# Stick-breaking attention on Trainium2: a scan over sigmoids with queries in rows, in place of triangle products with keys in rows

## The reference, cut to what matters

```python
def stick_breaking_mixer(x, w_in, w_out):
    q, k, v, g = jnp.split(x @ w_in, 4, axis=-1)          # 16 heads x 64 each
    ...
        z = jnp.einsum('bqhd,bshd->bhqs', qb, k) * HEAD_DIM_2 ** -0.5
        before = pos[None, :] < pb[:, None]
        log_one_minus = jnp.where(before, jax.nn.log_sigmoid(-z), 0.0)
        log_stick = lax.cumsum(log_one_minus, axis=3, reverse=True) - log_one_minus
        a = jnp.where(before, jnp.exp(jax.nn.log_sigmoid(z) + log_stick), 0.0)
        return jnp.einsum('bhqs,bshd->bqhd', a, v)
    ...
    return (o * jax.nn.silu(g)) @ w_out
```

## Time and profile before

| what | value |
|---|---|
| time, median of 3 runs | 1710.23 us (1708.13 to 1712.81) |
| time of the profiled execution | 1712.11 us |
| its span, first to last instruction | 1710.3 us |
| TensorE busy | 1618.1 us, 95% |
| VectorE, ScalarE, GpSimd busy | 873.2, 560.6, 547.1 us |
| TensorE's mean granted clock | 0.978 of full |

### The profile page before, as it was taken

One profiled execution on the slowest core, in us unless ns is written; L12 is line 12 of the kernel. 1 busy time (PEld: TensorE's weight loads), 2 busy tenths in 40 slices (PEclk: granted clock), 3 DMA queues, 4 the chain that ended last, 5 costly groups with the idle time before them and its releaser, 6 DMA issues.

```text
span 1710.3 us, 19912 instructions
## 1 busy us (share of the span) xinstructions
PE 1618.1 (95%) x7794; PEld 1317.4 (77%) x7794; DVE 873.2 (51%) x1604; ACT 560.6 (33%) x1165; POOL 547.1 (32%) x662
## 2 busy tenths in 40 slices
PE   6999999889999899999999998999989898999997
PEld 5888888677777788888788776877777686888885
DVE  2999957356643333333201134984772523655545
ACT  3223341455521222222100013015662205656550
POOL 3222235211124344444444441441102241222221
PEclk9999999899999899999999998999999999999999
DMA  8999988523359688888888884884315584554555
GB/s 232 191 192 190 195 189 192 104 59 75 75 116 225 152 183 190 192 194 193 173 192 177 177 190 85 188 194 86 71 30 135 122 190 95 111 111 99 111 115 131
DMA packets 69277, 253.15 MB, mean 148 GB/s; under 512 B 7616, under 2 KB 7744, under 8 KB 69184
## 3 DMA queue, kind: packets, MB, share of 16 engines
q0 software_dynamic: 66528, 242.25, 66.1%
q1 hardware_dynamic: 2112, 7.53, 1.2%
q10 hardware_dynamic: 544, 2.10, 0.3%
HBM read 249.75 MB, written 2.10 MB: 147 GB/s over the span
## 4 chain that ended last, share of the span: by engine, by line
PE 87%; DVE 5%; ACT 3%; DMA 2%; issue 2%; POOL 0%; SPq 0%; DVEq 0%; ACTq 0%
PE PSUM L426 26%; PE PSUM L428 26%; PE PSUM L427 26%; PE PSUM L707 2%; PE PSUM L586 2%; DMA W_LO<-wstream 2%; PE PSUM L607 2%; PE PSUM L689 1%; PE PSUM L692 1%; DVE MASK L1711 1%; PE PSUM L574 1%; DMA SMALLS<-small 1%; ACT PROBS L927 1%; PE PSUM L617 0%; ACT QKV L904 0%
## 5 line engine op out<-in xcount | busy, mean ns | idle before, releaser
L414 POOL DMA_DIRECT2D W_HI<-wstream x231 | 129.4, 560 | 1008.8 <-PE PSUM L428 1008.3
L426 PE MATMUL PSUM<-X_HI,W_HI 128*128 128x512 f32 x872 | 350.2, 402 | 8.8 <-DVEq L1775 3.6
L428 PE MATMUL PSUM<-X_HI,W_LO 128*128 128x512 f32 x872 | 343.1, 394 | 0.0
L427 PE MATMUL PSUM<-X_LO,W_HI 128*128 128x512 f32 x872 | 342.7, 393 | 0.0
L408 POOL DMA_DIRECT2D W_LO<-wstream x231 | 207.7, 899 | 104.8 <-POOL W_LO L405 84.2
L426 PE MATMUL PSUM<-W_HI,X_HI 128*128 128x512 f32 x544 | 214.5, 394 | 7.8 <-DMA W_LO<-wstream 4.3
L405 POOL TENSOR_SCALAR W_LO<-W_HI 128x1024 fp32r<-128x1024 f32 x195 | 211.8, 1086 | 21.6 <-DMA W_HI<-wstream 18.2
L427 PE MATMUL PSUM<-W_LO,X_HI 128*128 128x512 f32 x544 | 213.6, 393 | 0.0
L428 PE MATMUL PSUM<-W_HI,X_LO 128*128 128x512 f32 x544 | 213.2, 392 | 0.0
L426 PEld LDWEIGHTS PSUM<-X_HI,W_HI 128*128 128x128 f32 x872 | 165.9, 190 | 47.3 <-issue 10.9
L428 PEld LDWEIGHTS PSUM<-X_HI,W_LO 128*128 128x128 f32 x872 | 165.1, 189 | 36.0
(11 more groups left out here) (234 smaller groups left out, 2712.2 us busy)
## 6 DMA issues: line engine op xcount, KB each, us to landing
W_HI<-wstream POOLq DMA_DIRECT2D x231, 512.0 KB, 4.1
W_LO<-wstream POOLq DMA_DIRECT2D x231, 512.0 KB, 6.0
GATE_A<-x SPq DMA_DIRECT2D x4, 512.0 KB, 6.0
GATE_B<-x SPq DMA_DIRECT2D x1, 2048.0 KB, 17.1
NORM_GAINS<-lnv ACTq DMA_DIRECT2D x2, 1024.0 KB, 5.7
out<-GATE_B SPq DMA_DIRECT2D x3, 512.0 KB, 2.6
CONST<-consts SPq DMA_DIRECT2D x1, 968.0 KB, 10.8
out<-GATE_B SPq DMA_DIRECT2D x2, 256.0 KB, 2.0
```

The costliest lines, as they stand in the source:

```text
L414: pool.dma_start(W_HI[:, n % SLOTS, :], wstream[n]).then_inc(w_hi_in[n % SLOTS], 16)
L426: pe.matmul(o, lh, rh, start=start, stop=False)
L427: pe.matmul(o, lh, rl, start=False, stop=False)
L428: return pe.matmul(o, ll, rh, start=False, stop=stop)
```

## The change

Queries now stand in rows and keys along the free axis. For query block q of 128 rows, the scores against the first (q+1)*128 keys lie in one bank per head, and the mask is made of 64-row pieces. ScalarE takes sigmoid(-z) and sigmoid(z). VectorE runs one scan per head from the last key to the first, a running product in place, and multiplies the weights with it shifted by one. TensorE turns the weights by an identity, ScalarE and VectorE split them, and the values follow. The sums over triangles, the logarithms and the softplus are gone. The gate is one sigmoid out of PSUM. Whole slabs stand between the parts in bank 6, by a table of quarters per query block. The first slab goes ahead of the first scores, and the last turns and values go between slabs of the output projection. Before its first copy of a slab ScalarE waits for the layer norm to be done, since the norm's gains now share memory with the turned weights.

```diff
+STICK_FILL = 6 * [[4, 4, 0, 4]] + [[4, 4, 0, 0], [4, 2, 0, 2]]
+STICK_QUARTERS, STICK_SLABS = quarters(STICK_FILL, 0)
...
 # TensorE
-                def sums(i, h):
...
+                def fill(i, q):
+                    for n, part in STICK_QUARTERS[i, q]:
+                        slab_quarter(n, part, s0, SLAB_BANK, t0 + n if n else t0 - 4)
+                def scores(i, q):
+                    par, n, c = i % 2, (q + 1) * P, slice(q * P, (q + 1) * P)
+                    if q == 0:
+                        after(pe, "c_qk_lo", 2 * i + 2)
+                    after(pe, "c_taken", 4 * i + q - 1)
+                    for part in range(3):
...
+                            pe.matmul(PSUM[:, SCORE_BANK[q % 2][h], 0:n], l[d, par, 0, c], r[d, par, 1, 0:n],
+                                      start=part == 0, stop=False, skip_group_check=True)
+                    for half in range(2):
+                        for h in range(2):
+                            d, at = slice(h * HD, (h + 1) * HD), q * P + half * HD
+                            mm = pe.matmul(PSUM[:, SCORE_BANK[q % 2][h], at:at + HD], TRIANGLE[d, 1 + half, :], TRIANGLE[d, 0, d],
+                                           start=False, stop=half == 1, skip_group_check=True)
...
+                def turn_w(i, q):
+                    after(pe, "c_weights", 4 * i + q + 1)
+                    after(pe, "c_wt_lo", 4 * i + (0, 0, 2, 3)[q])
...
+                            mm = pe.transpose(PSUM[:, bank, at + kb * P:at + (kb + 1) * P], TAKEN[:, h, k:k + P], ident)
...
+                fill(0, 0)
+                pe.wait_ge(tile_free, t0)
                 for i in range(PAIRS):
+                    scores(i, 0)
                     if i:
+                        turn_w(i - 1, 2)
+                        fill(i, 0)
+                    scores(i, 1)
+                    if i:
+                        turn_w(i - 1, 3)
+                    fill(i, 1)
+                    scores(i, 2)
+                    fill(i, 2)
+                    if i:
+                        values(i - 1)
+                    turn_w(i, 0)
+                    turn_w(i, 1)
+                    scores(i, 3)
+                    fill(i, 3)
+                turn_w(PAIRS - 1, 2)
...
+                pe.wait_ge(sem("c_taken"), 4 * PAIRS)
+                t_half(0, s0, KT, O_HI, O_LO, t0 - 1, ready, slabs=(0,))
+                turn_w(PAIRS - 1, 3)
+                t_half(0, s0, KT, O_HI, O_LO, t0 - 1, ready, slabs=(1,))
                 values(PAIRS - 1)
+                t_half(0, s0, KT, O_HI, O_LO, t0 - 1, ready, slabs=(2, 3))
...
 # ScalarE
+            def taken(i, q):
...
+                act.activation(rest(q)[:, :, 0:n], z, ACT.Sigmoid, scale=-1.0).then_inc(sem("c_left"), 1)
+                after(act, "c_wturned", u - 3)
+                act.activation(TAKEN[:, :, at:at + n], z, ACT.Sigmoid).then_inc(sem("c_taken"), 1)
...
 # VectorE
+            def weights(i, q):
+                u, n, at = 4 * i + q, (q + 1) * P, PROB_AT[q]
+                r = rest(q)
+                after(dve, "c_left", u + 1)
+                for h in range(2):
+                    dve.tensor_tensor_scan(r[:, h, n - 1::-1], r[:, h, n - 1::-1], zero[:, 0:1].to_broadcast([P, n]), 1.0,
+                                           ALU.mult, ALU.add).then_inc(sem("c_rest"), 1)
+                after(dve, "c_rest", 2 * u + 2)
+                after(dve, "c_taken", u + 1)
+                w = TAKEN[:, :, at:at + n - 1]
+                dve.tensor_tensor(w, w, r[:, :, 1:n], ALU.mult).then_inc(sem("c_weights"), 1)
```

More of the change, by code:

```diff
@@ L512, in slab @@
                     mm.then_inc(slab_done, 1)
-                for n in range(kts // 2 - (2 if tokens else 0)):
+                for n in slabs or range(kts // 2 - (2 if tokens else 0)):
                     if aside and n == aside[0]:
@@ L673, in stick_attention @@
                 s0, t0 = SLAB0["stick"], TILE0["stick"]
[L675 to L694, removed]
@@ L1259, in _, with slabs @@
-            act.preload_act_table_set("natural_log_exp_and_others")
+            def slabs(i, q):
+                for n in slabs_done(STICK_QUARTERS, i, q):
+                    pair, kind = (n // 3, n % 3) if n < 3 * PAIRS - 3 else (PAIRS - 1, 2)
+                    if kind < 2:
+                        stick_qk_hi(pair + 1, kind, s0 + n, SLAB_BANK)
+                    else:
+                        act.wait_ge(slab_done, s0 + n + 1)
+                        act.activation(GATE_A[:, pair, :], PSUM[:, SLAB_BANK, :], ACT.Sigmoid).then_inc(sem("c_gate"), 1)
@@ L1260, in _ @@
+            act.wait_ge(sem("normed"), TT)
+            slabs(0, 0)
             for i in range(PAIRS):
-                last = i == PAIRS - 1
-                logs(i, 0)
+                taken(i, 0)
                 if i:
-                    gate(i - 1)
-                logs(i, 1)
-                stick_v_hi(i)
-                if not last:
-                    stick_qk_hi(i + 1, 0, s0 + 3 * i, STICK_SLAB_BANK)
+                    wt_hi(i - 1, 2)
+                    slabs(i, 0)
+                taken(i, 1)
+                if i:
+                    wt_hi(i - 1, 3)
+                slabs(i, 1)
+                taken(i, 2)
+                slabs(i, 2)
+                wt_hi(i, 0)
+                wt_hi(i, 1)
+                taken(i, 3)
@@ L1269, in _ @@
                 if i:
                     stick_out_hi(i - 1)
-                if i == 0:
-                    stick_qk_hi(i + 1, 1, s0 + 3 * i + 1, STICK_SLAB_BANK)
-                stick_weights(i, 0)
-                if i and not last:
-                    stick_qk_hi(i + 1, 1, s0 + 3 * i + 1, STICK_SLAB_BANK)
-                if last:
-                    gate(i)
-                stick_weights(i, 1)
+                slabs(i, 3)
+                stick_v_hi(i)
+            wt_hi(PAIRS - 1, 2)
@@ L1882, in constants @@
         "chunk": np.where((p // CHUNK) < (s[:, :P] // CHUNK), BIG, 0.0),
-        "nbig": np.where(p < s[:, :P], 0.0, -BIG),
-        "ntri": np.where(p >= s[:, :P], -1.0, 0.0),
+        "nbig": np.concatenate([np.where(p % HD + half * HD < s[:, :P], 0.0, -BIG) for half in range(2)], axis=1),
     }
```

228 lines of the change are left out of this document (91 added, 137 removed).

## The result

The changed kernel takes **1671.38 us** (median of 4 runs, 1668.74 to 1672.32), the kernel before 1709.18 (4 runs, 1706.60 to 1712.81): ratio 0.9775, 95% interval 0.9753 to 0.9797, a gain of 37.8 us. The prediction said 1676.6 in 1667 to 1693, and faster.

A forecast was written before the change was run, and what follows sets the result against it. TensorE's work and waits were taken to bound the kernel. Terms 43.5 - 20.4 + 2.4 + 9.8 - 1.0 - 0.7 = 33.6 us gained put the median at 1676.6 us, from 1710.2, range 1667 to 1693.

The forecast's parts named there:

- Sums, 43.5: Triangle sums leave TensorE: 16 heads x 2.72 us, all on the path, 43.5 us gained.
- Turns, -20.4: TensorE gets 20 turns of the weights per pair, 2.55 us a pair, 20.4 us lost over eight pairs.
- New waits at the bank, -0.7: TensorE waits 0.1 us for the slab's bank between a pair's fill 3 and the next fill 0: 0.7 us lost.
- Masks, +2.4: Smaller mask matmuls on TensorE, 0.25 us a block, 0.3 a pair after switches of form: 2.4 us gained.
- Switches, -1.0: Switches between the pieces on TensorE give back up to 1 us.
- Start and end, +9.8: Waits and low clock at the stage's start, in pair 0 and at its end go: 9.8 us gained.
- The scan: VectorE's scan of 512 elements taken at 0.68 us like a two-input operation; eight scans 3.9 us a pair.
- 2.1 us of slack at block 3: After block 3's scores VectorE is done 2.1 us before the slab's copy is asked; 0.7 by the half-throughput rule.
- Late VectorE: Rival: scans make VectorE late at the bank handover, 1 to 2 us a pair come back, 1689 us; chance 0.21.
- The bound for the slower side: Slower from about 4.8 us of wait and lost clock per pair, that is scans of about 5 ns an element.
- that rival: Scans at RECIPROCAL's rate: VectorE needs 32 us a pair; 1714 us, or 1732 with low clock; chance 0.04 each.
- Masks all but free: Rival: 64-row mask pairs run short side by side, no handover wait, 6 to 9 us more gained, 1669 us; chance 0.11.

The follow-up runs named there:

- the version with differences: Changed kernel with weights as differences of running products, no second sigmoid, masking in the scan, scores moved ahead of fills: 1665.88 us, ratio 0.9737 to the kernel before.

## Why the prediction was right, point by point

- *Sums, 43.5.* Right as a term of this change, wrong as I argued it. "All on the path" held only because something else stood in their place; alone, in the kernel before, 32 of the 40 products of each pair were worth 9.4.
- *Turns, -20.4.* Nearly right, as measured, with the hidden waits in it: all groups of turns together take 20.5. But ahead of a slab whose bank is free six turns take 0.63 us and eight 0.82, where I had 0.81 and 0.93 from rows in which scores or other products follow: 17.7 in all.
- *New waits at the bank, -0.7.* The handover was right to the hundredth, 1.95 us from the start of the slab's last product (1507.60 - 1505.65 in the run without masks). What stands inside was too long in my sum by the turns: 0.95 us passes for 0.63 at block 0 and 0.94 for 0.82 at block 1, so some 2.8 us wait in all, and not only at fill 0. The two errors, in turns and waits, cancel. What I did not see is that at this edge masks, turns and any later saving are worth nothing by themselves.
- *Masks, +2.4.* **The step that was mis-sized.** Scores with masks take 3.28 us a pair for 4.03: 0.75 a pair, 6.0. I took 0.25 a block and gave back for switches; they cost 0.16.
- *Switches, -1.0.* Slabs take 16.93 a pair for 16.74, values 3.89 for 3.77: -2.5.
- *Start and end, +9.8.* By distances of starts it was 10.7: 2.3 ahead of the first score, 6.7 from there to the second slab, 1.7 at the end. (I had counted the low clock wrongly: the first scores take 6.36 us to the next start, not 6.57, but the low level reached 0.6 into the slab behind them.) Two waits, 0.37 and 0.30, are left, 0.8 by starts: +9.9.
- Together 43.5 - 17.7 - 2.8 + 6.0 - 2.5 + 9.9 = 36.4. Added up over the whole stage instead of from one pair (distance to the next start, less the waits that the trace prints), it closes: sums 43.7, turns with hidden waits -20.5, scores with masks 8.4, slabs, values and projections -1.3, printed waits 6.6, together the 36.9 within 0.2. So the sum came out 3 us short mainly by the masks; that turns and hidden waits cancelled was luck.
- *VectorE.* The scan was chosen too fast: 7.1 us a pair instead of 3.9, so VectorE works 17.3 of 26.76 us, not 14.7. Of 2.1 us of slack at block 3 there were 1.03, between my choice and the 0.7 that the Trainium skill's rule gave. That was enough, so the time didn't move.
- *The rivals.* Late VectorE didn't come, but it was near: a second scan brings it. The bound for the slower side, scans of about 5 ns an element, held in the number: with each scan issued twice (2 x 2.36 = 4.7 ns an element at 512) the stage is 284.6 us for the 284.2 of before, and at 7.1 ns it is 44.4 slower. In part that is luck. The bound asks for 4.8 us a pair; the full pairs lost 3.9, and 10.9 came from the last pair and the output projection, which the bound left out. Nor was VectorE full, as that rival has it; it was late at one place. "Masks all but free", 1669, was half right: cheap masks, but with the handover still there.

## What to carry to other kernels

Where one buffer is handed over between two long pieces of an engine's work, the work between them isn't worth its length: up to the handover's time (here 1.6 to 1.7 us from the end of the first piece) it is cover, and only what exceeds it can be saved. Before costing a removal, list for each handover what stands inside; before adding one, move work in from places that have too much. An engine's busy share tells nothing of its room: VectorE was busy 65% of a pair and had 1 us to give.

## What the runs showed of the hardware that I had not expected

- Four 64-row products of 64 columns add 0.14 to 0.20 us to a group of scores, about half of what two 128 x 128 ones took (0.34, from 4.03 less the 2.65 of scores without masks, over four blocks).
- What a group of turns costs depends on what follows: six take 0.63 us ahead of a slab whose bank is free and 0.77 to 0.81 ahead of scores.
- A scan costs 1.21 us for 512 elements and 2.1 ns for each element between 128 and 512; reading its second operand from a table or broadcast makes no difference (1211 and 1212 ns for 512), nor does max for add.
- GpSimd's negation and a VectorE operation that reads SBUF alone stretch each other, as in the earlier trace rows: 1.52 for 0.68 us beside 1.63 for 1.06; in the version with differences only VectorE's is stretched, 1.72 for 0.69. Whether it happens hangs on a shift of a microsecond, so a delay may grow by 0.8 to 1.0 us as it moves.
- Behind a wait of 2.43 us in each pair the granted clock was at its lower level for about 3 us (0.50 from 1495 to 1498); behind waits of 0.72 us twice a pair it stayed at 1.00.
